# Gate projections by seven products of half blocks instead of eight, with gate values and attention rows parked in DRAM

## The reference, cut to what matters

```python
z = rms_norm(x) @ w_in                      # q, k, v, u, vs, ga, gb; ga and gb have 1024 columns each
oa = attention(q, k, v)                     # windowed, 512 wide
ob = gelu(u) * (W_spatial @ layer_norm(gelu(vs)) + b)      # 512 wide
h  = sigmoid(ga) * (oa @ w_branch_a) + sigmoid(gb) * (ob @ w_branch_b)
y  = x + h @ w_out
y += mixture_of_experts(rms_norm(y))        # 16 experts, 2 per token
```

## Time and profile before

| | |
|---|---|
| time, three runs | 944.48 us median (942.85 to 944.61) |
| the profiled execution | 944.06 us, span 942.0 us |
| mean granted clock of TensorE | 0.988 |
| busy: PE, PEld | 899.2 us (95%), 805.4 us (85%) |
| busy: DVE, ACT, POOL | 458.5 us (49%), 358.0 us (38%), 227.2 us (24%) |

### The profile page before, as it was taken

How to read it: one execution, slowest core, us unless ns; L and a number is a source line. 1 busy time by engine, 2 the same in 40 slices (tenths; PEclk the granted TensorE clock), 3 DMA queues, 4 the chain that set the end, 5 groups by cost and what they waited for, 6 DMA issues and landing times. The chain is left out here.

```text
span 942.0 us, 16172 instructions
## 1 busy us (share of the span) xinstructions
PE 899.2 (95%) x5389; PEld 805.4 (85%) x5390; DVE 458.5 (49%) x827; ACT 358.0 (38%) x623; POOL 227.2 (24%) x242
## 2 busy tenths in 40 slices
PE   8999998999999999999999999999789999999993
PEld 7777776887999999999999999999678888888882
DVE  5777877343222222221231245443887758577550
ACT  5666655210232111121121132222526757576641
POOL 2444221345220000000000010000152456464561
PEclk9999999999999999999999999999999999999997
DMA  7321311200302102001111015973539888979733
GB/s 247 113 67 53 117 51 31 62 0 1 104 1 77 59 33 66 34 33 67 33 38 62 22 58 177 346 256 95 186 113 314 301 284 294 334 240 333 234 52 45
DMA packets 57360, 118.57 MB, mean 126 GB/s; under 512 B 7470, under 2 KB 32750, under 8 KB 57297
## 3 DMA queue, kind: packets, MB, share of 16 engines
q1 hardware_dynamic: 49824, 100.10, 30.9%
q0 software_dynamic: 7488, 17.85, 8.3%
HBM read 105.37 MB, written 23.00 MB: 136 GB/s over the span
## 5 line engine op out<-in xcount | busy, mean ns | idle before, releaser
L1408 ACT ACTIVATE gate<-psum 128x352 f32<-128x352 f32 x48 | 22.4, 466 | 209.9 <-PE psum L79 209.9
L77 PE MATMUL psum<-w_hi,hT_hi 128*128 128x512 f32 (+3 forms) x224 | 82.9, 370 | 3.6 <-issue 1.9
L2188 DVE TENSOR_TENSOR hT_lo<-room,hT_hi (+1 forms) x32 | 72.1, 2290 | 17.2 <-ACT hT_hi L1881 17.2
L77 PE MATMUL psum<-hT_hi,x_xT_hi 128*128 (+1 forms) x192 | 77.9, 406 | 1.2 <-DVE x_xT_lo L2343 0.9
L79 PE MATMUL psum<-w_hi,hT_lo 128*128 128x512 f32 (+3 forms) x224 | 78.9, 352 | 0.0
L78 PE MATMUL psum<-w_lo,hT_hi 128*128 128x512 f32 (+3 forms) x224 | 78.8, 352 | 0.0
L77 PE MATMUL psum<-hT_hi,w_hi 128*128 128x352 f32 x240 | 77.4, 323 | 0.0
L78 PE MATMUL psum<-hT_lo,w_hi 128*128 128x352 f32 x240 | 76.9, 321 | 0.0
L79 PE MATMUL psum<-hT_hi,w_lo 128*128 128x352 f32 x240 | 76.9, 320 | 0.0
L78 PE MATMUL psum<-hT_lo,x_xT_hi 128*128 (+1 forms) x192 | 75.8, 395 | 0.0
L79 PE MATMUL psum<-hT_hi,x_xT_lo 128*128 (+1 forms) x192 | 75.7, 394 | 0.0
(11 more groups left out here) (351 smaller groups left out, 2300.4 us busy)
## 6 DMA issues: line engine op xcount, KB each, us to landing
room<-in_w_gu SPq DMA_DIRECT2D x16, 2048.0 KB, 11.1
dn_raw<-in_w_dn SPq DMA_DIRECT2D x16, 1024.0 KB, 7.0
g_w_raw<-in_w_ab SPq DMA_DIRECT2D x15, 768.0 KB, 4.4
xT_chunk<-in_xT SPq DMA_DIRECT2D x8, 528.0 KB, 3.8
x_in<-in_x SPq DMA_DIRECT2D x8, 512.0 KB, 3.4
out_y<-y SPq DMA_DIRECT2D x8, 512.0 KB, 3.3
hn_rows<-squares SPq DMA_DIRECT2D x8, 512.0 KB, 3.2
o_w_raw<-in_w_out_t SPq DMA_DIRECT2D x7, 512.0 KB, 6.8
```

Of the source, the lines that this page charges most:

```text
L77: eng.matmul(out, lh, rh, start=first and k == 0, stop=False)
L1408: act.activation(gate[:, (ab + c) % 2, :], bank(psum, gate_pair(ab, c))[:, 0:TC], ACT.Sigmoid).then_inc(gated.sem, 1)
L2188: dve.tensor_tensor(gu_lo[:, buf, ks], gu_raw[:, buf, ks], gu_hi[:, buf, ks].bitcast(F32), ALU.subtract).then_inc(gu_lo_made.sem, 1)
```

## The change

Gates. Let `hT` be cut into four quarters (k: model rows 0 to 511 and 512 to 1023; tokens 0 to 527 and 528 to 1055), and the gate weights of a pair of output blocks into four as well. Of ga and gb together there are 8 such turns. A turn's four quarters of results come from seven products instead of eight (Strassen's form). Each product is two chunks of 264 tokens (HC) with four blocks of contraction, 24 matmuls. Four of the moving operands are sums of quarters, `T1` to `T4`, formed once and split; POOL forms four sums of weights in each turn, and DVE adds up the results from PSUM.

Room. The T's take the place of `oaT` and of a quarter of `hT`, so the attention rows are stored to DRAM at the end of the attention phase and come back after the last gate product. The gate values (after the sigmoid) go to DRAM quarter by quarter and come back for the branches, which now follow all the gates: 8 pieces of ob, then 8 of oa. Half of the first `w_out` piece (FIRST_K, 4 of 8 blocks) is done at the end of the block. The block boundary between u and gates is gone, loops are written out, and the last u chunk goes in four units of 264 tokens, the later tokens first.

The diff, cut (`wait_ge` lines partly left out):

```diff
+HALF = NTOK // 2
+HC = HALF // 2
+FIRST_K = KD // 2
 def attention_phase(nc, io, keep, psum):
@@ sync
+            sp.wait_ge(oa_lo_made, NT)
+            for o, name in zip(oaT, ("oa_hi", "oa_lo")):
+                sp.dma_start(io[name], o[:, :, :].rearrange("p k n -> p (k n)").bitcast(F32)).then_inc(oa_stored, DMA)
...
+            sp.wait_ge(oa_stored, 2 * DMA)
-def sgu_gate_phase(nc, io, keep, psum):
-def gates_phase(nc, io, keep, psum):
+def dense_phase(nc, io, keep, psum):
+    UNITS = [(q, slice(c * TC, (c + 1) * TC)) for q in range(KE - 1) for c in range(3)]
+    UNITS += [(KE - 1, slice(c * HC, (c + 1) * HC)) for c in (2, 3, 0, 1)]
+    SUMS = ("A11", "S2", "S3", "A12", "S1", "A22", "S4")
+    SLOTS = 5
+    Y_BANKS = (0, 1, 2, 3, 4)
+        MOVING = (quarter(0, 0), T[2], T[3], quarter(1, 0), T[1], T[4], quarter(1, 1))
+        X_BANKS = (0, 1, 5, 6, 7, 2, 3, 4)
@@ sync
+            for q in (1, 2):
+                load_u(q)
+            for used in keep["used"]:
+                sp.sem_clear(used)
+            load_u(3)
+            (two halves of the weights of turns 0 and 1)
+            for n in range(TURNS):
+                load_weights(n + 2)
+                store(n, 2, 0, 0, e1, c11_out)
+                if n == TURNS - 1:
+                    for v in range(4):
+                        load_sig(v)
+                store(n, 4, 1, 1, out, c22_out)
+                store(n, 6, 1, 0, u3, c21_out)
+                store(n, 8, 0, 1, out, c12_out)
+            load_weights(TURNS + 2)
+            sp.wait_ge(m_made, passed(GATES - 1))
+            for o, name in zip(oaT, ("oa_hi", "oa_lo")):
+                sp.dma_start(o[...], io[name]).then_inc(oa_in, DMA)
+            sp.dma_start(first_o_raw.rearrange("p k c -> p (k c)"), io["w_out_t"][0]).then_inc(out_in, DMA)
+            for v in range(4, BRANCHES):
+                load_sig(v)
@@ gpsimd
+            for u in range(US):
+                ob_low(u)
+                if u < 6:
+                    third_sum(u % 2, u // 2)
+                if u == US - 3:
+                    for name in ("S1", "S2", "S3"):
+                        weight_sum(0, name)
+            fourth_sum()
+            weight_sum(0, "S4")
+            for n in range(1, TURNS):
+                for name in ("S1", "S2", "S3", "S4"):
+                    weight_sum(n, name)
+            for v in range(KD, BRANCHES - 1):
+                pool.wait_ge(multiplied, 3 * v + 3)
+                pool.tensor_tensor(here, here, part[v % 2], ALU.add).then_inc(h2_summed, 1)
@@ scalar
+            for u in range(US):
+                if u in (0, 3, 6):
+                    u_high(u // 3 + 1)
+                u_step(u)
+                if u in (4, 5):
+                    t_high(1, u - 4)
+                if u in (6, 7):
+                    t_high(2, u - 6)
+                    t_high(3, u - 6)
+                if u in (9, 10):
+                    high(u - 9)
+            high(2)
+            high(3)
+            fourth_high(t_raw[3], slice(2, 4))
@@ tensor
+                if n == 0 and summed:
+                    pe.wait_ge(t_lo[summed - 1], 2)
+                for c in range(2):
+                    ... product(pe, x_of(g, c), ..., KH).then_inc(m_made, 1)
+            pe.wait_ge(out_hi, 2)
+            for k in range(FIRST_K):
+                pe.wait_ge(h2_lo, k + 1)
+                (three chunks of the first w_out piece)
@@ vector
+            def first_sum(piece, stage):                  # 128 x 2 x 528 elements a pass
+                raw = T_raw[1][:, 2 * piece:2 * piece + 2]
+                if stage == 0:
+                    t.did(dve.tensor_tensor(raw, h12, h11, ALU.subtract))
+                elif stage == 1:
+                    t.did(dve.tensor_tensor(raw, raw, l12, ALU.add))
+                else:
+                    dve.tensor_tensor(raw, raw, l11, ALU.subtract).then_inc(t_raw[0], 1)
+            for u in range(US):
+                if u in (0, 3, 6):
+                    u_low(u // 3 + 1)
+                u_step(u)
+                if u < 3:
+                    for piece in range(2):
+                        first_sum(piece, u)
+                if u in (3, 4):
+                    second_sum(u - 3)
+                if u in (5, 6):
+                    t_low(1, u - 5, u - 4)
+                if u in (7, 8):
+                    t_low(2, u - 7, u - 6)
+                    t_low(3, u - 7, u - 6)
+                if u in (9, 10):
+                    low(u - 9)
+                if u == US - 3:
+                    fourth_sum(0)
+                if u == US - 2:
+                    fourth_sum(1)
+                    fourth_sum(2)
+            low(2)
+            low(3)
+            t_low(4, 1, 1)
+            for g in range(GATES):
+                gates(g)
+                if g == 2:
+                    t_low(4, 0, 2)
+                low(g + SLOTS - 1)
 def merge_moe_phase(nc, io, keep, psum):
-            for k in range(KD):
-                wait(pe, h2_lo, k - LATE + 1)
+            for k in range(FIRST_K, KD):
```

More of the change, by code:

```diff
@@ L37 @@
 TC = NTOK // 3
-EARLY = ((0,), (1,), ())
-LATE = sum(len(ks) for ks in EARLY)
+HALF = NTOK // 2
+HC = HALF // 2
+FIRST_K = KD // 2
+ARENA = SG * NTOK + 4 * KD * P + 2 * (KD // 2) * HALF + 4 * TC + 2 * (KD // 2) * P
 NG, EPG = 4, 4
@@ L248, in attention_phase @@
         oT_made, oa_hi_made, oa_lo_made = sem("oT_made"), sem("oa_hi_made"), sem("oa_lo_made")
[L249 removed]
+        k_out_made, oa_stored = sem("k_out_made"), sem("oa_stored")
         kv_stored = sem("kv_stored")
@@ L1163, in _ @@
             add_bias(PT)
-def sgu_gate_phase(nc, io, keep, psum):
[L1169 to L1291, removed]
-            ob_made.begin(dve)
-            dve.sem_inc(w_lo_made.sem, 1)
-            def low(q, j):
-                raw, hi, lo = weights[j]
-                w_hi_made.wait(dve, q)
-                u_made.wait(dve, 3 * q - 4)
-                dve.tensor_tensor(lo[:, :, :], raw[:, :, :], hi[:, :, :].bitcast(F32), ALU.subtract).then_inc(w_lo_made.sem, 1)
-            def step(q, j):
-                next_chunk(q, j, low)
-                if is_last(q):
-                    dve.wait_ge(first_hi_made, 1)
-                    dve.tensor_tensor(first_g[2][:, :, :], first_g[0][:, :, :], first_g[1][:, :, :].bitcast(F32),
-                                      ALU.subtract).then_inc(first_lo_made, 1)
-                for c in range(3):
-                    u, b = 3 * q + c, (j + c) % 2
-                    u_gelu.wait(dve, u)
-                    lo_made.wait(dve, u - 2)
-                    dve.tensor_tensor(ob[:, b, :].unsqueeze(1), u_act[:, b, :].unsqueeze(1),
-                                      mixT[:, bass.ds(q, 1), c * TC:(c + 1) * TC], ALU.mult).then_inc(ob_made.sem, 1)
-            over_chunks(dve, step)
@@ L1872, in keep_y @@
                 ins.then_inc(y_copied, 1)
-            for k in range(LATE, KD):
-                act.activation(hT[0][:, k, :], h2[:, k, :], ACT.Copy).then_inc(h2_hi, 1)
             for f in (gu_hi_made, dn_hi_made, xT_hi_made, silu_made, hidT_hi_made, out_made):
@@ L2192, in _ @@
                 f.begin(dve)
-            for k in range(LATE, KD):
-                dve.wait_ge(h2_hi, k - LATE + 1)
-                dve.tensor_tensor(hT[1][:, k, :], h2[:, k, :], hT[0][:, k, :].bitcast(F32), ALU.subtract).then_inc(h2_lo, 1)
             dve.memset(y[:, PT, :], 0.0).then_inc(zeroed, 1)
@@ L2419, in hybrid_layer @@
         with ExitStack() as dense:
+            with ExitStack() as short:
+                sb(short, "ahead_of_hT_lo", [P, KD, NTOK])
+                keep["hT_lo_raw"] = sb(short, "hT_lo_raw", [P, KD, NTOK])
             for name in ("hT_hi", "hT_lo"):
@@ L2516 @@
     io["hn"] = nc.dram_tensor("hn_rows", (NTOK, D), F32, kind="Internal").ap()
+    io["sig"] = nc.dram_tensor("gate_rows", (2, KD, P, NTOK), F32, kind="Internal").ap()
+    for name in ("oa_hi", "oa_lo"):
+        io[name] = nc.dram_tensor(name, (P, KE * NTOK), F32, kind="Internal").ap()
     hybrid_layer(nc, io)
```

589 lines of the change are left out of this document (425 added, 164 removed).

## The result

The changed kernel takes 950.52 us (median of four runs, 950.25 to 950.83), the kernel before 944.55 us beside it (942.85 to 944.79): the ratio is 1.0069, with a 95% interval of 1.0053 to 1.0085. It is slower by 0.7%. Measured again on another chip, unchanged, it took 947.87 against 943.39 us, 1.0049 (1.0032 to 1.0067). The profiled execution of the first measurement took 950.56 us, with a span of 948.8 and a mean clock of 0.978.

A forecast was written before the change was run, and what follows sets the result against it. PE was taken to bound u, gates and branches, with DVE and POOL, queued one after another, delaying its startup: 944.1 - 21.2 + 23.3 + 0.7 + 3.6 = 950.5 us, range 932 to 958.

The forecast's parts named there:

- PE's work: -21.2: U chunks, gates and branches: fewer matmul columns on PE and no inner block boundary, best case 21.2 us saved.
- short matmuls save nothing: Rival, gates: at 0.136 us a matmul the 1344 cost what the 1152 did, 969 us; chance 0.03.
- DVE bounds the gates: Rival, gates: DVE sets the pace; at 22 us a turn the time is 962 us; chance 0.07.
- The startup: +23.3: U stretch until product six: DVE and POOL run one after another forming the T's, PE waits 23.3 us, bounds 18 to 31.
- +0.7 for the clock behind the last gap: Behind the startup's last PE gap: the granted clock falls to its lower level, costing 0.7 us.
- my 2.0: Start of the u block: an earlier weight load brings the first u low part from 244.59 to 242.6.
- my 76.2: First u low part to product six: 74.2 us of DVE and POOL queues added, plus some 2 us idle.
- Parked data: 0: Attention rows and gate quarters stored to DRAM and loaded back: transfers hidden, 0 us.
- 0.6 + 2.4 that I allowed: Branches of the second half: a 0.6 us DVE part may wait up to 2.4 us behind POOL's h2 sum, costing PE 0.
- The end of the block: +3.6: Last branch to second w_out piece: its low weights wait for the constants and the clock falls, 3.6 us lost, bounds 0 to 5.
- 17.5 plus a share of the clock: Last branch's end to second w_out piece: 17.5 us, plus 1.4 for the lower clock, 18.9 against 15.3 now.
- 2.2 + 1.4: End of the block: the 3.6 us in two parts, 1.4 of it for a clock that falls again.

The follow-up runs named there:

- Experiments 1: Changed kernel with T3's six passes moved from POOL to DVE: 943.4 us against 943.76 of the kernel before, ratio 0.9998.
- experiment 2: Changed kernel with POOL's six T3 passes replaced by twelve memsets that only write, so T3 is zero: 942.89 us (one run).
- experiment 5: Changed kernel with T3 and T4's near half on DVE and the second w_out piece split before the constants' wait: 936.04 us against 944.4, ratio 0.9911.
- Experiment 4: Changed kernel with DVE splitting the second w_out piece before it waits for the constants: 944.78 us against 943.76 of the kernel before, ratio 1.0024.
- experiment 8: Changed kernel with the whole first w_out piece behind the block boundary (FIRST_K = 0): 948.71 us against 944.4 of the kernel before, ratio 1.0047.
- experiment 12: Changed kernel, all T sums on DVE, early w_out split, earlier weight sums, T1 formed in attention but not beside the last tile: 928.23 us, ratio 0.9828.
- experiment 7: Changed kernel, all T sums on DVE (T1 and T2 in the attention block), early w_out split, weight sums one unit earlier: 929.31 us, ratio 0.9839.

## Why the prediction was right

I said 950.5 us, slower by 0.6%, and it is 950.5. That it hits so closely is luck: the same kernel took 947.9 on another chip. Sign and mechanism are not; I take them by the places that I forecast, in the first profile.

**PE's work: -21.2, right.** The two rows 27 instructions apart give (333.10 - 329.82)/27 = 0.1215 us for 264 columns (0.122 from a line through 256 and 352). From product six to the end of the last branch, at 560.7, lie 240.9 us; 241.0 forecast. Nothing waits in the turns, so the rivals "short matmuls save nothing" and "DVE bounds the gates" are out.

**The startup: +23.3, right in place and size; +0.7 for the clock behind the last gap, not seen.** Product six starts at 319.81, forecast 318.8 on a scale on which PE starts the block 0.39 us earlier. From the block's start it is 82.15 us for PE's own 58.2: 23.9 lost. The waits are where I said: the third and fourth u chunk, products two, three, five and six. Experiments 1 and 2 show the cause and its sign, and most of the price: from the first u low part on, six passes less on POOL and six more on DVE save 5.9 us, and six that read nothing save 12.7, so a pass costs the pair some 2.1 us on POOL (2.4 forecast) and 1.1 on DVE. The forecast took this from rows, and the Trainium skill's rule that it cited (SBUF — State Buffer, "Who interferes with whom"), that the one that issues first blocks the other fully, agrees with this case's 2.69 us for a 352-column product that takes 0.52 alone.

Behind product six nothing is lost to the clock: it is granted 1.00 from 318 to 560, and the 240.9 us are PE's own work. The 0.7 is made up by the startup, 23.9 for 23.3. Inside it two small terms are off, in opposite directions. The first u low part starts at 243.98, 1.0 us earlier than before when that shift is counted, for my 2.0; by the other three profiles of this startup that term lies between 0.9 and 2.6. From there to product six it is 75.83 us for my 76.2: in 73.3 of them at least one of the two engines is at work, where the sum said 74.2, and in 2.5 both are idle, where I took 2. The unheld POOL pass takes 2.40 us, as estimated.

The weak point, which experiment 5 found, is what belongs to the sum. It counts what product six needs; but POOL goes on to work that nobody needs yet, and that holds DVE as well.

**Parked data: 0, right.** The two loads of the attention rows take 9.2 and 13.8 us for 2112 KB each, far inside the 45.8 us of cover, and a store of a gate quarter 2.1. No PE wait in the branches. Some of DVE's low parts last 2.95 us there beside POOL's h2 sum, which is the 0.6 + 2.4 that I allowed, and the banks of PSUM take it.

**The end of the block: +3.6, right in sum (+3.5), its terms mis-sized.** The boundary costs 0.30 us, not 2.1, since the other engines arrive while PE still has its half piece. `bias` is issued 2.2 us behind the boundary's matmul as before, so the second piece comes 16.1 us behind the last branch, where I had 17.5 plus a share of the clock, and the gap ahead of it is 4.06 us, not 2.4. Behind this longer gap the granted clock is 0.50 from 576.78 to 582, its lower level (before: 1.00 from 573 to 578), and from the second piece to the router matmul PE needs 7.6 us instead of 4.9: 2.7 for my 1.4. Together 0.8 + 2.7, for 2.2 + 1.4. Experiment 4 takes the gap away, experiment 8 shows the exchange.

**The account.** Until the last branch's end 2.9 us more (560.7 for 557.75), until the router matmul 3.5 more, after it 0.3 more, less 0.3 outside the span: 6.5, which is 950.56 less 944.06.

What stays open. The two profiled executions of the changed kernel differ by 3.4 us: 1.6 in the load ahead of the first u low part, 1.0 between product six and the router matmul, all of it behind the second w_out piece, the rest before and after; why the load takes 1.7 us more in some executions no run shows. In experiment 12 product six still comes 6 us behind PE's own work. From the first u low part to there (58.78 us) both engines are idle together for 1.2 only, so the sum of the two queues is again the likely bound; no run takes POOL's weight sums of turn 1 out of it.

## What to carry to other kernels

Before sharing elementwise work between VectorE and GpSimd, add up, over the stretch that feeds the matrix engine, all instructions of both that read two operands (VectorE) or anything (GpSimd) from SBUF: in this kernel they went one after another. Count the work too that an engine will take up early because it has become free. In such a stretch a pass is cheapest on the engine that does it fastest, here VectorE at half the time, even when GpSimd is idle. Work that is moved into an engine's idle time in an earlier stage is free only if the other engine reads nothing there, and if it isn't the last thing ahead of a boundary. Move a piece of work across a boundary only after asking which of the waits behind it, a constant's load for instance, it had covered.

## What the runs showed of the hardware that I had not expected

- The holding reaches far smaller instructions than those moved: a 352-column product on DVE went from 0.52 to 2.69 us beside POOL's 1056-column pass, and both engines look busy all the while. Busy time of such a pair (64.4 and 51.0 us of 83) says little of the work done.
- A memset of 1056 columns on POOL takes 0.98 us beside DVE's passes (experiment 2) and 0.98 and 0.99 in the attention stage of the kernel before, against 2.40 for a tensor-tensor pass of that length.
- The cost of a held instruction depends on who is late: beside the last token tile (experiment 7) two DVE passes added 1.5 and 0.9 us to POOL's steps, beside the others they delayed DVE's own next step by 0.64.
